# Two gaps of 128 bytes shift where the weight operands of 10,144 matmuls begin in SBUF

## The reference

```python
def hybrid_layer(x, p_i, positions, ...):
    h = rmsnorm(x, norm_mix)
    z = h @ w_in                       # 1024 x 3336
    y_ret, y_pool, y_ml = retention(...), pool_mix(...), mlstm(...)
    x = x + jnp.concatenate([y_ret, y_pool, y_ml], axis=-1) @ w_out
    h = rmsnorm(x, norm_ffn)
    gu = h @ w_gate_up                 # 1024 x 5632
    x = x + (jax.nn.silu(gu[..., :D_FF]) * gu[..., D_FF:]) @ w_down
    hp = rmsnorm(x, norm_ple)
    x = x + jax.nn.sigmoid(hp @ w_ple_gate) * (p_i @ w_ple_proj)
    return x
```

## Time and profile before

| | |
|---|---|
| Time, median of 3 runs | 2496.57 us (2496.37, 2496.57, 2498.0) |
| Span of the profiled execution, first to last instruction | 2494.5 us |
| Median less span: what lies around the span | 2.1 us |
| TensorE matmul busy | 2467.6 us, 99% |
| TensorE weight load busy | 2037.2 us, 82% |
| VectorE, ScalarE, GpSimd busy | 1270.7, 898.2, 992.5 us |
| Granted TensorE clock, mean | 0.998 |

### The profile page before, as it was taken

One profiled execution on the slowest core, in us unless ns is written; L12 is line 12 of the kernel. 1 busy time (PEld: TensorE's weight loads), 2 busy tenths in 40 slices (PEclk: granted clock), 3 DMA queues, 4 the chain that ended last, 5 costly groups with the idle time before them and its releaser, 6 DMA issues.

```text
span 2494.5 us, 29698 instructions
## 1 busy us (share of the span) xinstructions
PE 2467.6 (99%) x11768; PEld 2037.2 (82%) x11768; DVE 1270.7 (51%) x1760; ACT 898.2 (36%) x1298; POOL 992.5 (40%) x596
## 2 busy tenths in 40 slices
PE   7999999999999999999999999999999999999998
PEld 6888888888888888888878887888888888888886
DVE  7967845543343352333596777545433433423335
ACT  4333334433333341125333252344433333322253
POOL 3211112278877832321221121223788877222120
PEclk9999999999999999999999999999999999999999
DMA  4342222123223252211143322311232223422111
GB/s 164 105 98 65 71 85 85 45 84 92 76 77 91 87 195 107 78 50 44 38 154 98 78 56 67 102 59 60 80 93 81 76 85 110 150 110 70 51 49 70
DMA packets 89370, 214.43 MB, mean 86 GB/s; under 512 B 34568, under 2 KB 43016, under 8 KB 84880
## 3 DMA queue, kind: packets, MB, share of 16 engines
q1 hardware_dynamic: 61456, 126.90, 16.9%
q10 hardware_dynamic: 27776, 85.63, 10.0%
HBM read 163.70 MB, written 35.68 MB: 80 GB/s over the span
## 4 chain that ended last, share of the span: by engine, by line
PE 97%; DVE 1%; ACT 1%; issue 0%; DMA 0%; POOL 0%; ACTq 0%; DVEq 0%; POOLq 0%
PE proj L1986 20%; PE proj L1987 20%; PE proj L1988 20%; PE proj L2090 5%; PE aux L2090 5%; PE aux L2089 5%; PE proj L2089 5%; PE aux L2088 5%; PE proj L2088 5%; PE aux L2205 1%; PE aux L2224 1%; PE aux L2215 1%; PE aux L2310 0%; PE aux L2315 0%; PE aux L2281 0%; PE aux L2268 0%
## 5 line engine op out<-in xcount | busy, mean ns | idle before, releaser
L1937 POOL TENSOR_TENSOR w_lo<-w_raw,w_hi 128x1024 fp32r<-128x1024 f32 (+1 forms) x144 | 367.2, 2551 | 1256.5 <-ACT w_hi L1468 1256.4
L1986 PE MATMUL proj<-h_hi,w_hi 128*128 128x512 f32 x1760 | 694.8, 395 | 0.9 <-POOL w_lo L1937 0.9
L1988 PE MATMUL proj<-h_lo,w_hi 128*128 128x512 f32 x1760 | 685.5, 389 | 0.0
L1987 PE MATMUL proj<-h_hi,w_lo 128*128 128x512 f32 x1760 | 685.1, 389 | 0.0
L1986 PEld LDWEIGHTS proj<-h_hi,w_hi 128*128 128x128 f32 x1760 | 330.4, 188 | 72.4 <-issue 3.1
L1988 PEld LDWEIGHTS proj<-h_lo,w_hi 128*128 128x128 f32 x1760 | 330.3, 188 | 69.2
L1987 PEld LDWEIGHTS proj<-h_hi,w_lo 128*128 128x128 f32 x1760 | 330.5, 188 | 68.8 <-issue 2.4
L1468 ACT ACTIVATE w_hi<-w_raw 128x1024 fp32r<-128x1024 f32 (+1 forms) x143 | 146.5, 1026 | 440.5 <-PE proj L1988 295.9
L1025 DVE TENSOR_TENSOR x<-x,proj 128x512 f32<-128x512 f32 x128 | 87.7, 687 | 405.6 <-PE proj L1988 405.3
L1944 POOL TENSOR_TENSOR w_lo<-w_raw,w_hi 128x512 fp32r<-128x512 f32 x120 | 183.5, 1531 | 88.5 <-ACT w_hi L1450 88.5
L1944 POOL TENSOR_TENSOR w_lo<-turns,w_hi 128x512 fp32r<-128x512 f32 x120 | 180.4, 1504 | 62.9 <-ACT w_hi L1450 62.9
(11 more groups left out here) (290 smaller groups left out, 4161.3 us busy)
## 6 DMA issues: line engine op xcount, KB each, us to landing
w_raw<-weights SPq DMA_DIRECT2D x168, 512.0 KB, 3.7
act_spill<-act ACTq DMA_DIRECT2D x44, 512.0 KB, 5.5
turns<-weights SPq DMA_DIRECT2D x40, 512.0 KB, 4.4
h_whole<-act_spill ACTq DMA_DIRECT2D x12, 1024.0 KB, 8.1
ffn_b_whole<-act_spill ACTq DMA_DIRECT2D x8, 1024.0 KB, 5.5
w_raw<-weights SPq DMA_DIRECT2D x16, 384.0 KB, 3.1
ml_d<-rows_spill ACTq DMA_DIRECT2D x64, 64.0 KB, 3.4
rows<-ret_qkv ACTq DMA_DIRECT2D x32, 128.0 KB, 2.3
```

Source lines behind the costliest of these rows:

```text
L1937: g.tensor_tensor(wlo[:, slot, 0:n], w, whi[:, slot, 0:n].bitcast(F32), ALU.subtract).then_inc(weights_ready.sem, 1)
L1986: pe.matmul(out, wh, rhi, start=first, stop=False)
L1987: pe.matmul(out, wl, rhi, start=False, stop=False)
L1988: return pe.matmul(out, wh, rlo, start=False, stop=final)
```

## The change

Two unused tiles of 32 float32 (128 bytes in each partition) are allocated, one ahead of `w_hi` and one ahead of `w_lo`. Nothing else is edited.

```diff
         raw = sb("w_raw", [P, 2, 1024])
+        sb("w_hi_gap", [P, 32])
         whi = sb("w_hi", [P, RING, 1024], F32R)
+        sb("w_lo_gap", [P, 32])
         wlo = sb("w_lo", [P, RING, 1024], F32R)
```

## The result

The changed kernel takes 2559.64 us (median of 4 runs, 2559.47 to 2559.73) against 2496.53 us, a ratio of 1.025 with a 95% interval of 1.0236 to 1.0265: 63 us slower, where no change was forecast.

What follows compares the result with a forecast made beforehand. The prediction took TensorE's own matmul stream to bound the kernel. All terms were 0 us: 2494.5 + 0 = 2494.5 us, with the 2.1 us around it 2496.6 us; range 2440 to 2514 us, chance 0.83.

Steps and rivals of the forecast that it cites:

- What bounds the kernel: Whole kernel: TensorE's own stream sets the time, busy 99% of 2494.5 us; its waits add up to 16.1 us.
- The price list: All 10,144 matmuls reading w_hi or w_lo: 1 ns more on each step is 10.1 us, or 0.41%.
- starting 128 or 256 bytes further on changes the order of the collisions and hardly their number: Weight loads beside float32r matmuls: each load passes through every phase up to 1 KB, so 0 ns a step, 0 us.
- The four starts that I had compared: Weight operands in the FFN at 0, 512, 1024, 1536 bytes past a multiple of 2048: one pace, 0.2267 us a step.
- The loss bound: Float32r steps: at worst the 232.2 ns seen behind a float32 stretch, 5.6 ns x 10,144 = 57 us.
- a loss of more than two cycles a step: Float32r steps: the part of the slower case beyond two cycles of 0.83 ns each, chance 0.07.
- Rival 2: Float32r steps: slower, a shifted load outlasts the matmul hiding it; 2505 to 2514 us, or 2553; slower had chance 0.15.
- Float32 rows as evidence: Float32 matmuls at half the moving rate: shifted weights showed no effect of addresses, so neither gain nor loss was favoured.
- Writers, const, par, turns, rows: ScalarE and GpSimd writes to shifted w_hi and w_lo, and tiles 256 bytes further on: 0 us each.
- Rival 1: Float32r steps: faster, distinct phases unlock colliding reads; 2381 us if all goes, 2458 in part; faster had chance 0.23.
- the 13.3 ns left over at phase 0: Float32r step of 226.7 ns, less 213.3 ns for 512 columns at one column a cycle of 2.4 GHz.
- The rule cited ahead of the result: TensorE's two SBUF reads: independent ports for moving operand and weight loads, so no collision exists and the sum is 0.

Runs made afterwards that it cites:

- e11: TensorE streams alone, none of the kernel's work: weights at 16 bytes run after different streams, 226.7 ns a step behind phase 0, 233.3 behind phase 8.
- e1: TensorE streams alone, none of the kernel's work: 32 matmuls a line at varied operand phases, types and widths; float32r 226.7 ns at phase 0, 232.4 with weights at 128.
- e5: Kernel before, with the whole arena 128 bytes later, so moving operands, high and low weights all shift alike: 2496.67 us, ratio 1.0000.
- e7: Kernel before, with low weight parts (w_lo) alone 128 bytes past a multiple of 2048: 2539.58 us, ratio 1.0171.
- e2: Kernel before, with only what lies behind w_lo (const, par, rstd, turns, rows and the rest) 256 bytes later: 2496.45 us, ratio 0.9999.
- e3: Kernel before, with low weight parts at 256 bytes past a multiple of 2048, const and the rest as in the changed kernel: 2496.42 us, ratio 0.9999.
- e8: TensorE streams alone, none of the kernel's work: 48 matmuls a line, weights at finer phases from 0 to 256 bytes, and fewer columns; 226.7 ns reached at 0 and 256.

## Why the prediction was wrong

The forecast of 2496.6 us and the range up to 2514 missed 2559.6 us.

- *What bounds the kernel.* Right. No wait appeared, and the difference is the step of TensorE's stream times 10,144, but for the 4 us accounted for above. The price list (1 ns is 10.1 us) was right too.
- *"starting 128 or 256 bytes further on changes the order of the collisions and hardly their number".* This is the step that failed. It took both reads to run on at a pace of their own, whatever happened between them, so that only the number of collisions counted, and put the change of the step at 0. Measured, it is 6.6 ns a step. e11 shows that the pace isn't fixed even at one set of addresses, where what ran before makes it 226.7 or 233.3 ns. e1 and e5 show that whether the fast rhythm is found depends on the distance at the start, modulo 256. The four starts that I had compared (0, 512, 1024, 1536) are all the same phase in that period, so their one pace, read as a sign that phase doesn't matter, was no test of it.
- *The loss bound.* The rows of the answer were there: nine steps of 232.2 ns behind a float32 stretch, priced at 57 us and 2553 us. I wrote that this was "not an effect of addresses" and gave a loss of more than two cycles a step 0.07. Such steps are what a stream runs before it settles (e11, L70), and with the shift it never settles: 233.3 ns and 63 us. That both are one state isn't shown, only that their paces lie within 1.1 ns of each other. Rival 2 had the side and nearly the price; its mechanism, a load that takes longer than its cover, was wrong, as loads stay at 188 ns in the trace (2039.3 us for 11,768 against 2037.2) and the start that crosses a multiple of 2048 is no slower than the rest.
- *Float32 rows as evidence.* They stayed as they were, as predicted (e1 L111 and L112, L2251 of the changed kernel, and e7, where `par` moved by 128 and the step is 429 ns still), and they don't stand for float32r. The text named this as the part most likely to fail, and it did.
- *Writers, const, par, turns, rows.* 0 us was right (e2: 2496.45 us). So was 0 for the low parts (e3), but by luck: 256 is a whole period, while 128 alone costs 43 us (e7). Nothing in the prediction told the two apart. The 256 bytes that `const` and `par` moved are a whole period too.
- *Rival 1*, that the 13.3 ns left over at phase 0 can be unlocked, has nothing for it: of the 37 phases tried in e8 none is below 226.7 ns, and the three phases of the changed kernel made the step longer. What those 13.3 ns are stays open. Loading fewer weight columns doesn't shorten them, and bfloat16 hasn't got them.

The rule cited ahead of the result, from the Trainium skill's page "TensorE: Matmul & The Clock Gate" (section "What happens when you issue a matmul"), says that loading the next weights takes no read bandwidth from the running matmul. Float32 agrees with it, 429 ns at 0 and at 128 (e1, L111, L112). Float32r doesn't: with weights at 128 in place of 0 a bare stream's step goes from 226.7 to 232.4 ns, and moving both operands together brings it back (L67, L72, L87), so there the two reads are not independent of each other. Where the rule and this measurement differ, the measurement decides.

What in SBUF repeats every 256 bytes, and why 120 behaves like 0, the runs don't show. Neither do they show which of the two reads waits.

## What to carry to other kernels

For float32r products of 512 columns that load weights for every matmul, put weights and moving operands a multiple of 256 bytes apart in the partition and check the step from start to start in the timeline, as the busy share (99% before and after) and the modelled durations (0.39 and 0.40 us) show next to nothing of it. At other widths measure first: at 256 columns the price was gone. When equal paces at several addresses are to prove that addresses don't matter, ask first which periods these addresses can tell apart: four starts 512 bytes apart say nothing on a period of 256. And a short stretch in the trace that runs slower than the rest with no wait is a state that the hardware can be in, so its pace belongs in the range, and with a chance above the 0.07 that it had here.

## What the runs showed of the hardware

- A float32r stream has more than one steady pace at the same addresses, and keeps the one that it has: 226.7 or 233.3 ns for at least 96 matmuls (e11, L67 and L69).
- Distance in bytes between weights and moving operand, and settled step in ns: 0, 256, 512: 226.7; 120: 226.7; 192: 228.9; 128: 232.4; 32: 233.3; 96: 234.3; 28: 235.0 (e1, e8, single starts). Off 0 the pace can also depend on what ran before: 16 has 226.7 or 233.3.
- A shifted operand lengthens two steps, the one beside its load and the one that runs on it: 232.8 and 234.0 ns against 226.6 (e1, L93).
- bfloat16 takes 216 ns for 512 columns, a settled float32r stream never less than 226.7, in the same kernel (e1). Neither bfloat16 nor float32 has a price at 128.
- At 256 columns float32r has 120.0 ns at phase 0 and 118.8 at 128 (e1, L105, L106). Streams of 192 and of 128 columns both have 111.7 at phase 0 (e8, L112, L111).
